# Three small pads in the on-chip memory, which move the streamed tiles to another place relative to the weights

## The reference, cut to what matters

```
for i in range(DEPTH):                       # first kind, DEPTH = 2
    z = rmsnorm(x, g_mix[i]) @ w_in[i]       # 2048 -> 4928
    ...                                      # attention, two convolutions, retention
    x = x + concatenate([y_a, y_b, y_c, y_d]) @ w_o[i]
    uf = causal_dwconv(rmsnorm(x, g_ffn[i]) @ w_up[i], w_ffn_conv[i])   # 2048 -> 2 * 5632
    gate, up = split(uf, 2)
    x = x + (silu(gate) * up) @ w_down[i]    # 5632 -> 2048
    x = x + (p[i] @ w_pe[i]) * sigmoid(rmsnorm(x, g_pe[i]) @ w_pg[i])   # p: 256 -> 2048
for l in range(DEPTH):                       # second kind
    p = rms_norm(x, norm_g[l]) @ w_in[l]     # four attention variants and their gates
    x = x + mixed @ w_out[l]
```

## Time and profile before

| | |
|---|---|
| time, median of 3 | 3403.39 us (3398.33 to 3408.09) |
| profiled execution | span 3398.6 us |
| TensorE busy | 3366.2 us, 99%, 20334 matmuls |
| weight loads busy | 2929.1 us, 86% |
| VectorE, ScalarE, GpSimd busy | 77%, 45%, 25% |
| HBM | 600.80 MB read, 177 GB/s |

### The profile page before, as it was taken

The page is one execution under the profiler, slowest core; times in us unless marked ns, Lnnn a source line. Parts: engine busy times, 40 slices in busy tenths (PEclk is TensorE's granted clock), DMA queues, the critical chain, the costliest instruction groups (busy, mean ns, idle before and its releaser), DMA issues. The chain is left out here.

```text
span 3398.6 us, 53679 instructions
## 1 busy us (share of the span) xinstructions
PE 3366.2 (99%) x20334; PEld 2929.1 (86%) x20334; DVE 2614.4 (77%) x3392; ACT 1531.5 (45%) x1642; POOL 862.4 (25%) x633
## 2 busy tenths in 40 slices
PE   8999999999999999999999999999999999999998
PEld 7988888888888889888888888888888888888887
DVE  8887788787786878886887787867867866677865
ACT  5654443343433555544443433435444444444443
POOL 0332323122122423314322120214422003150004
PEclk9999999999999999999999999999999999999999
DMA  6445555555555554455555555555544445544454
GB/s 236 148 150 174 186 185 186 176 205 173 199 178 187 203 177 165 137 174 186 185 186 172 201 180 202 174 187 197 193 166 149 165 171 186 178 162 149 167 179 149
DMA packets 90647, 605.21 MB, mean 178 GB/s; under 512 B 10192, under 2 KB 10352, under 8 KB 29296
## 3 DMA queue, kind: packets, MB, share of 16 engines
q1 hardware_dynamic: 89424, 599.83, 51.6%
q10 hardware_dynamic: 1056, 3.11, 0.3%
HBM read 600.80 MB, written 2.10 MB: 177 GB/s over the span
## 5 line engine op out<-in xcount | busy, mean ns | idle before, releaser
L634 PE MATMUL bank<-H,whi 128*128 128x512 f32 x6496 | 2295.3, 398 | 15.2 <-DVE H L1667 13.2
L638 PE MATMUL bank<-H,wlo 128*128 128x256 f32 x6624 | 1857.5, 280 | 0.0
L1145 ACT ACTIVATE whi<-raw 128x2048 fp32r<-128x2048 f32 (+2 forms) x609 | 1093.6, 1796 | 1106.9 <-DMA raw<-in_slabs_down 264.7
L1611 DVE TENSOR_TENSOR wlo<-raw,whi 128x2048 fp32r<-128x2048 f32 (+2 forms) x609 | 1327.1, 2179 | 246.2 <-ACT whi L1145 239.8
L634 PEld LDWEIGHTS bank<-H,whi 128*128 128x128 f32 x6496 | 1217.7, 187 | 311.6 <-issue 20.8
L638 PEld LDWEIGHTS bank<-H,wlo 128*128 128x128 f32 x6624 | 1251.6, 189 | 0.7
L634 PE MATMUL bank<-G,whi 128*128 128x512 f32 x1408 | 493.3, 393 | 0.0
L508 POOL TENSOR_TENSOR sqtmp<-tmp 128x256 f32<-128x256 f32 x88 | 219.0, 2489 | 880.5 <-DVE tmp L2191 880.5
L638 PE MATMUL bank<-G,wlo 128*128 128x256 f32 x1408 | 392.9, 279 | 0.0
L634 PEld LDWEIGHTS bank<-G,whi 128*128 128x128 f32 x1408 | 263.8, 187 | 63.0
L638 PEld LDWEIGHTS bank<-G,wlo 128*128 128x128 f32 x1408 | 263.8, 187 | 0.0
(11 more groups left out here) (387 smaller groups left out, 2876.5 us busy)
## 6 DMA issues: line engine op xcount, KB each, us to landing
raw<-in_slabs_up SPq DMA_DIRECT2D x176, 1024.0 KB, 4.9
raw<-in_slabs_down SPq DMA_DIRECT2D x128, 704.0 KB, 4.0
raw<-in_slabs_wo SPq DMA_DIRECT2D x32, 1024.0 KB, 4.9
raw<-in_slabs_pg SPq DMA_DIRECT2D x32, 1024.0 KB, 4.9
raw<-in_slabs_gates SPq DMA_DIRECT2D x32, 1024.0 KB, 4.9
raw<-in_slabs_wout SPq DMA_DIRECT2D x32, 1024.0 KB, 4.9
raw<-in_slabs_sc SPq DMA_DIRECT2D x24, 1024.0 KB, 4.8
raw<-in_slabs_fox SPq DMA_DIRECT2D x24, 1024.0 KB, 5.0
```

What stands on the lines that cost most here:

```text
L634: pe.matmul(b[0:r.m, :], whi[:, n % RAW, w], r.src[:, k, :], start=at == 0, stop=False)
L638: last = pe.matmul(b[0:r.m, 0:T], wlo[:, n % RAW, w], r.src[:, k, 0:T], start=False, stop=at == r.kt - 1)
L1145: act.activation(whi[:, n % RAW, 0:w], raw[:, n % RAW, 0:w], ACT.Copy).then_inc(S("hi_ready"), 1)
L1611: dve.tensor_tensor(wlo[:, n % RAW, 0:w], raw[:, n % RAW, 0:w], whi[:, n % RAW, 0:w].bitcast(F32), ALU.subtract).then_inc(S("lo_ready"), 1)
```

## The change

Three tensors that nothing reads or writes are put between the others. 48 floats (192 bytes) go ahead of `H` and 80 floats (320 bytes) behind it, together 512. 24 floats (96 bytes) go ahead of the area of z, y, `cq` and `G`.

```diff
     x = sb("x", [P, DC, T])
+    sb("ahead_of_H", [P, 48])
     H = sb("H", [P, DC, 2 * T], F32R)
+    sb("behind_H", [P, 80])
     area_raw = nc.sbuf_tensor("raw", [P, RAW, 2048], F32)
     raw = area_raw.__enter__()
     area_raw.__exit__(None, None, None)
...
     small = sb("small", [P, T])
     small2 = sb("small2", [P, T])
 
+    sb("ahead_of_z", [P, 24])
     area = nc.sbuf_tensor("z", [P, 32, T], F32)
```

## The result

| | before | changed |
|---|---|---|
| time, median | 3403.39 us (3398.33 to 3408.09, 5 runs) | 3416.12 us (3414.86 to 3419.36, 5 runs) |
| ratio | | 1.0038, 95% interval 1.0026 to 1.0050 |
| span of the profiled execution | 3398.6 us | 3417.2 us |

The change makes the kernel slower by 0.4%, 12.7 us between the medians; the forecast was 144 us less. The two profiled spans differ by 18.6 us. The profiled execution after took 3419.36 us, the longest of its five, and its span is 2.2 us shorter than that, as in all runs here spans are some 2 us shorter than times; by that the one of before took about 3401 us, an estimate, somewhat under its median.

A forecast was written before the change was run, and what follows sets the result against it. TensorE's gapless matmul stream bounds the kernel: matmul count times start distance. Savings of 149.6 us from 3398.6, plus 5 for VectorE, gave 3254.0; adding the execution's 4.8 us shortfall to the median, 3259 us, range 3215 to 3335.

The forecast's parts named there:

- The 5 us for VectorE: Densest VectorE windows, four of 50 us: waits there give back between none and 11 us; 5 us taken.
- p's surcharge of 6.7 ns a load: p projection, 256 columns at 192: 113.3 ns less 106.7 for the columns; assumed for every streamed tile's load.
- The surcharge goes by the weight load, not by the column.: At distance 0: 13.3 ns for 256 or 512 columns, 26.7 for a pair with two weight loads.
- Matmuls of 256 columns: 864 on H, 384 at L636 to L638, 240 on cq: 6.7 ns less each, 10.0 us.
- Value slabs: 960 matmuls of 512 columns, distance -192: 6.7 ns less each, 6.4 us; 0 if only +192 is good.
- The comparison of p and cq: Same form and size, 113.3 against 120.0 ns; said to differ in tile position, 192 against 96 bytes off the weights.
- That the address matters: Weight loads reading memory while the matmul ahead streams from it would make beats depend on distance; inferred from p and cq.
- By the column: Rival: p's gain belongs to 256 columns, or pairs settle in another rhythm; pairs 340.0 ns, 3316 us; chance 0.16.
- The change does nothing: Rival: p is quick for another reason, its short unrolled stretch or what other engines leave alone; 3403 us; chance 0.08.
- The rival on the other side: Slower: pairs at 192 fall into group 0's worst step, about 0.36 us; 80 us more, 3483 us; chance 0.06.
- if the slow rhythm of 353.3 merely took over everywhere: Milder form of the slower rival: all pairs at 353.3 ns, 25 us more, 3428 us.
- What would show it wrong: Pairs at two or more rhythms above 340; cq at 120; or TensorE gaps with VectorE over 95% in named windows.

The follow-up runs named there:

- the run with z alone: Kernel before with only the 96-byte pad ahead of z, putting cq and G at 192; H, p and weights unmoved: 3414.83 us, ratio 1.0038.
- the three-matmul form at 192: Changed kernel with each 512-column matmul on H and G split into two of 256, each with its own weight load: 3393.31 us, ratio 0.9955.

## Why the prediction was wrong

- *What bounds the kernel.* Right: TensorE without gaps, before and after, VectorE at 77%, no new waits. The 5 us for VectorE never came up. The sum started from a span, 3398.6 us, and took all 4.8 us to the median as this execution's shortfall; some 2 us of them are the difference between a span and a time. That is nothing beside the miss.
- *The step that failed.* "I let every streamed tile take p's surcharge of 6.7 ns a load, so a pair costs 320.0 + 13.3 = 333.3 ns." A pair at 192 costs 353.3 ns, also behind extra matmuls of 12 widths. It failed twice over. p's 113.3 ns is one of two beats that 256 columns have at 192, and which one p takes changed with what ran ahead (113.3 behind G at 96, 117.8 behind G at 192, p untouched). And a beat of 256 columns does not carry over to a pair: the pair at 192 showed no quick one.
- *"The surcharge goes by the weight load, not by the column."* It fitted three rows at distance 0 (13.3, 13.3 and 26.7 ns), and it was already at odds with two that I listed beside them, 33.3 at the same distance and 30.0 on G at 96, where cq pays 13.3. At 192 a pair with two loads and a block with three both take 353.3.
- *The other terms that used p's surcharge.* Matmuls of 256 columns were to gain 6.7 ns each, 10.0 us in all; they mostly took the slow beat of 192, 117.8, and gained 2.2 ns, 3.7 us. Value slabs were to gain 6.4 us, or nothing at the worst; they went from 226.7 to 228.9 ns and lost 1.0 us.
- *The comparison of p and cq.* It was said that they differ only in where the tile lies. They differed in what ran ahead of them as well, and in the run with z alone p slowed to 117.8 although it had not moved.
- *That the address matters.* Right, with the wrong value. Moving the tiles changes pairs from 353.3 to 346.7, with the form and the order of the work the same. The rule of the Trainium skill, "SBUF — State Buffer", section "Who interferes with whom" (two independent read ports, TensorE never waits on anyone), would give one time for all distances; the runs give 3372 to 3422 us, so the measurement decides against what the forecast drew from the rule, that the time would stay. Whether the ports have a part in it, and what inside the chip makes the difference, no run shows.
- *The rivals.* "By the column" at 340.0 ns a pair did not come. "The change does nothing" is 12.7 us off in size, and that is outside the noise. The rival on the other side was right in its milder form: "if the slow rhythm of 353.3 merely took over everywhere", given as 25 us more, 12.7 measured. It had 7.9 us for the pairs in mixed slabs, which lost 3.8, and it left out what 256 columns gain.
- *What would show it wrong* was named: pairs above 340. But the sign that mattered most was in the rows of before. The same stream at the same addresses ran at 346.7 in one group and at 353.3 in another. That should have told me that an address does not fix the beat, p's least of all, on a stretch of 96 matmuls.

The quickest pair in any row of before was 346.7 ns, and a kernel with every pair at 346.7 takes 3372 to 3375 us, as three runs showed. The range ended at 3335 and so lay wholly below what any row had shown for a pair.

## What to carry to other kernels

Where matmuls run without gaps, the distance between their starts is a quantity to measure in each stage, since it can differ by 2 to 4% at the same shape: here between 346.7 and 353.3 ns for a pair and between 113.3 and 117.8 for 256 columns. Which beats a stream can take went by the distance between the streamed tile and the weights; which of two it took could be changed by what ran ahead of it, and no rule found here tells which one follows. If a stream shows two beats at the same addresses, no single stretch tells what a new place will give; try several pads in full-size runs. Here 32 and 160 bytes off the weights gave 0.9909 and 0.9921 of the time, better than both kernels, where 64, 192 and 224 gave 1.004 to 1.006.

## What the runs showed of the hardware

- A pair of matmuls with 768 columns took 346.7, 348.9, 350.0, 351.1 or 353.3 ns depending on where the streamed tile lay relative to the weights, in steps of 32 bytes. 512 bytes on everything from H upwards left the time as it was (ratio 1.0001), and so did 256 on H alone (1.0002), which changed the beat of one stage.
- At distances of 0 and 64 (pairs) and 192 (256 columns) the stream has two beats. In the undisturbed stretches of the profiles it kept the one it had through loops and slabs; in the three-matmul form at 192 one matmul of 128 columns turned it over in 12 of 14 cases.
- At 192 with three matmuls a block the executions of one kernel spread over 3334 to 3397 us, in heaps 27 to 33 us apart, while those of each kernel with pairs at 32, 128, 160, 192 or 224 stayed within 6 us of each other.
